# Input projection of a hybrid encoder kernel: from eight plain blocks to seven block products per set, with the steps between them reordered

## What is computed

```python
h = (_rmsnorm(x, g_mix) * (1.0 + scale1) + shift1).astype(dt)
proj = jnp.einsum('bsd,de->bse', h, w_in)
q, k, v, g_sw, p, gate_a, gate_b = jnp.split(proj, IN_SPLITS, axis=-1)
...
ret = ((ret - mu) * lax.rsqrt(var + EPS)).reshape(b, s, RET_V) * ret_gn_gain
branch_a = jax.nn.silu(g_sw) * ret
...
merged = jax.nn.sigmoid(gate_a) * branch_a + jax.nn.sigmoid(gate_b) * branch_b
mix_out = jnp.einsum('bsd,de->bse', merged.astype(dt), w_out)
x = x + gate1 * mix_out
...
up = _dwconv_centred(jnp.einsum('bsd,df->bsf', h2, w_up), conv_w, conv_b)
act, lin = jnp.split(up, 2, axis=-1)
return x + gate2 * jnp.einsum('bsf,fd->bsd', jax.nn.gelu(act) * lin, w_down)
```

## Time and profile before

| | us |
|---|---|
| median of 3 runs | 2647.01 (2646.71 to 2648.02) |
| span of the profiled execution | 2646.8 |
| TensorE busy in it | 2594.0 (98%) |
| DVE, ACT, POOL busy | 1659.9 (63%), 988.5 (37%), 1258.2 (48%) |
| the eight head pairs (all of `mix`) | 27.0 to 608.4 and 1337.8 to 1904.3 |

### The profile page before, as it was taken

One profiled execution on the slowest core, in us unless ns is written; L12 is line 12 of the kernel. 1 busy time (PEld: TensorE's weight loads), 2 busy tenths in 40 slices (PEclk: granted clock), 3 DMA queues, 4 the chain that ended last, 5 costly groups with the idle time before them and its releaser, 6 DMA issues.

```text
span 2646.8 us, 32184 instructions
## 1 busy us (share of the span) xinstructions
PE 2594.0 (98%) x12084; PEld 2131.5 (81%) x12084; DVE 1659.9 (63%) x2179; ACT 988.5 (37%) x1431; POOL 1258.2 (48%) x844
## 2 busy tenths in 40 slices
PE   7999989999999999999999999999999999999998
PEld 4888878888778888878878888888887888888886
DVE  3768686867786666665848273645768655555434
ACT  5211111114555454555621111111246545455443
POOL 1222333216377777655642122122453877775645
PEclk9999999999999999999999999999999999999998
DMA  7223153435134544497631212131251333325764
GB/s 297 91 88 125 48 197 112 150 112 154 58 128 147 167 168 158 157 337 238 184 122 49 70 33 85 33 92 43 81 147 32 104 120 104 103 93 180 213 193 146
DMA packets 300090, 341.01 MB, mean 129 GB/s; under 512 B 16288, under 2 KB 189728, under 8 KB 299936
## 3 DMA queue, kind: packets, MB, share of 16 engines
q1 hardware_dynamic: 297056, 328.46, 38.2%
q10 hardware_dynamic: 2880, 10.49, 1.0%
HBM read 263.39 MB, written 75.50 MB: 128 GB/s over the span
## 4 chain that ended last, share of the span: by engine, by line
PE 87%; DVE 5%; ACT 2%; DMA 2%; issue 2%; POOL 1%; SPq 1%; POOLq 0%; DVEq 0%; ACTq 0%
PE ps L921 26%; PE ps L890 23%; PE ps L1082 14%; PE ps L1247 11%; PE ps L977 5%; PE ps L1014 1%; PE ps L1275 1%; PE ps L1300 1%; PE ps L1299 1%; PE ps L1125 1%; PE ps L1312 1%; POOL y_sq L1823 1%; PE ps L1286 1%; DVE sq L2050 0%; ACT h_full L1492 0%
## 5 line engine op out<-in xcount | busy, mean ns | idle before, releaser
L1848 POOL TENSOR_TENSOR f_w<-f_ring,f_w 128x512 fp32r<-128x512 f32 x434 | 595.7, 1379 | 398.8 <-ACT f_w L1450 393.7
L921 PE MATMUL ps<-hc_hi,f_w 128*128 128x512 f32 x2240 | 690.5, 389 | 3.5 <-ACT u_act L1526 2.8
L1804 POOL TENSOR_TENSOR w_split<-w_raw,w_split 128x1024 fp32r<-128x1024 f32 x88 | 224.0, 2549 | 666.3 <-ACT w_split L1371 666.3
L890 PE MATMUL ps<-h_hi,w_split 128*128 128x512 f32 x1792 | 497.0, 394 | 6.9 <-ACT v_sb L1637 6.9
L921 PEld LDWEIGHTS ps<-hc_hi,f_w 128*128 128x128 f32 x2240 | 420.1, 188 | 92.7 <-ACT u_act L1526 3.7
L921 PE MATMUL ps<-hc_lo,f_w 128*128 128x512 f32 x1120 | 435.7, 389 | 0.0
L1082 PE MATMUL ps<-act_ring,f_w 128*128 128x512 f32 x1848 | 421.5, 390 | 3.6 <-DVE act_ring L2164 1.9
L1082 PEld LDWEIGHTS ps<-act_ring,f_w 128*128 128x128 f32 x1848 | 346.6, 188 | 77.5 <-issue 4.2
L890 PEld LDWEIGHTS ps<-h_hi,w_split 128*128 128x128 f32 x1792 | 334.2, 188 | 79.0 <-ACT v_sb L1637 7.5
L1450 ACT ACTIVATE f_w<-f_ring 128x512 fp32r<-128x512 f32 x434 | 269.9, 624 | 252.8 <-POOL f_ring L1858 109.7
L1247 PE MATMUL ps<-w_split,h_hi 128*128 128x512 f32 x1024 | 322.7, 396 | 5.5 <-DVE h_lo L2037 5.5
(11 more groups left out here) (210 smaller groups left out, 3296.7 us busy)
## 6 DMA issues: line engine op xcount, KB each, us to landing
f_ring<-in_w_up SPq DMA_DIRECT2D x160, 256.0 KB, 3.2
f_ring<-gated_out SPq DMA_DIRECT2D x154, 256.0 KB, 3.0
w_raw<-in_w_in SPq DMA_DIRECT2D x56, 512.0 KB, 3.9
gated_out<-gated_up SPq DMA_DIRECT2D x44, 512.0 KB, 4.1
f_ring<-down_sums SPq DMA_DIRECT2D x88, 256.0 KB, 3.0
gated_out<-t_gated SPq DMA_DIRECT2D x22, 768.0 KB, 6.0
f_ring<-in_w_down SPq DMA_DIRECT2D x66, 256.0 KB, 3.5
late_rows<-in_w_late SPq DMA_DIRECT2D x32, 512.0 KB, 5.6
```

Of the source, the lines that this page charges most:

```text
L890: ins = pe.matmul(ps[:, slot, b * HALF:(b + 1) * HALF], w[:, w_slot, col:col + P], a[:, k, b * HALF:(b + 1) * HALF], start=first and n == ...
L921: ins = pe.matmul(ps_row[:, half_of(bank)], a[:, cols], b, start=i in (0, 1, 3) and k == 0 and n == 0, stop=k == KQ - 1 and n == 2, skip_g ...
L1804: pool.tensor_tensor(w_lo[:, ws, :], w_raw[:, i % 2, :], w_hi[:, ws, :].bitcast(F32), ALU.subtract).then_inc(lo_done.sem, 1)
L1848: pool.tensor_tensor(piece_slot(q)[:, 1, :], piece_raw(q), piece_slot(q)[:, 0, :].bitcast(F32), ALU.subtract).then_inc(piece_lo.sem, 1)
```

## The change

The input projection is made in seven block products too, the order of everything in `mix` is rewritten around them, and weights and late rows are loaded otherwise.

1. *Gates.* GS, GA and GB become three *sets* (0: swish, 1: gate a, 2: gate b), each for both heads at once: the set's 256 output channels and the 1024 tokens are cut in 2x2 blocks, and seven products (`unit_product`, 12 matmuls of 512 columns each; (s, o) is product o of set s) take the place of 2 x 48 matmuls. Four products are copied out of PSUM by ACT (`copy_unit`: o = 0, 1, 2, 6; 512 columns), three are added on top by DVE (`unit_add(s, n)` after o = 3, 4, 5). The tanh is then taken from SBUF.
2. *q, k, v.* In pairs 1 to 3 of each sequence also in seven products (`qkv_products`, o = 0 to 6), 48 matmuls of 256 columns each; ACT copies four (`copy_qkv`), DVE adds three (`qkv_add`, 1024 columns). Rope then works on SBUF, in two halves (`rope_half`). In pair 0 q, k and v stay plain, and there the sums of blocks of h are made (`t_piece_low`, `t_piece_diff`, 2048 columns, DVE; `t_piece_high`, ACT).
3. *Order.* P comes right behind q, k, v; the turns of q and k behind P; the scores behind product (0, 0); the other small steps behind the products that the table `behind` names. DVE's and ACT's lists are rewritten in the same order.
4. *Weights.* 22 loads of 256 KB a pair through a ring of eight; 512-column pieces through five buffers; POOL also makes four sums of weight blocks per set. W_in comes with its columns permuted beforehand.
5. *Late rows.* Each sequence now sums its own 32 tiles, one instruction a tile, in its pairs 1 and 2, 16 tiles a pair, spread over six spots (`LATE_SPOTS`) of DVE's list; the ring has two buffers. Before, sequence 1 had none in its pairs.
6. *Around it.* x is loaded again ahead of `out` in both sequences, the first loads of `out` wait for the end of the last pair, and the block sums of w_out are made on POOL in pair 3 of sequence 0.

The core of the diff:

```diff
-LATE_RING = 4
-LATE_FROM = (0, 0, 10, 21, 32)
+LATE_RING = 2
+LATE_FROM = (0, 0, 16, 32, 32)
+LATE_SPOTS = (6, 3, 1, 2, 2, 2)
...
+            def late_load(seq, n):
                 if n >= LATE_RING:
-                    sp.wait_ge(late_sum, 2 * (n - LATE_RING) + 2)
+                    sp.wait_ge(late_sum, LATE_TILES * seq + n - LATE_RING + 1)
...
+                    for j in range(KC):
+                        mix_in(where, j)
...
+                    late = late_loads(late, 1)
+                    store_merged(("mix", seq, pr - 1))
+                    late = late_loads(late, LATE_SPOTS[0] - 1)
...
+                    for j in range(KC, KC + 4):
+                        mix_in(where, j)
...
+                    late = late_loads(late, sum(LATE_SPOTS[1:3]))
+                    for j in range(KC + 4, MIX_LOADS - 4):
+                        mix_in(where, j)
...
+            def qkv_products(where):
...
+                for o in range(PRODUCTS):
+                    i = ORDER_UP[o]
...
+                    elif o == 6:
+                        pe.wait_ge(*q_summed.at(where, 2))
+                    else:
+                        pe.wait_ge(*q_copied.at(where, {2: 1, 4: 3, 5: 2}[o]))
...
+                            rows, cols = slice(t * P, (t + 1) * P), slice(k2 * 2 * P, (k2 + 1) * 2 * P)
+                            k = 2 * kk + k2
+                            for n, (a, b) in enumerate(((high, w[0]), (high, w[1]), (low, w[0]))):
+                                ins = pe.matmul(ps[:, Q_SLOT[i], t * 2 * P:(t + 1) * 2 * P], a[:, k, rows], b[:, cols],
...
+            def pool_unit(where, between=None):
...
+                if pr:
+                    pe.wait_ge(*q_copied.at(where, 4))
...
+            def unit_product(where, s, o):
...
+                else:
+                    pe.wait_ge(*u_copied.at(where, 4 * s + {2: 1, 4: 3, 5: 2}[o]))
...
                     def branch_b(h):
                         slot = slot_of(where, f"BB{h}")
-                        if h == 0:
-                            pe.wait_ge(*cent_done.at(where, 1))
-                        else:
-                            pe.wait_ge(*sw_done.at(where, 2))
+                        pe.wait_ge(*ma_done.at(where, h + 1))
...
+                    if pr:
+                        qkv_products(where)
+                        pool_unit(where)
+                        turn_qk()
+                        behind = {(0, 2): (products, 0), (0, 4): (products, 1), (0, 6): (outputs, 0), (1, 3): (outputs, 1),
+                                  (1, 5): (turn_ret, 0), (2, 1): (branch_b, 0), (2, 3): (turn_ret, 1), (2, 4): (branch_b, 1)}
...
+            def copy_unit(where, s, o):
...
+                elif (s, o) == (2, 1):
+                    act.wait_ge(*ga_done.at(where, 2))
...
+                    def unit_add(s, n):
...
+                        dve.wait_ge(*used.at(where, set_piece(pr, s, 3 + n) + 1))
+                        dve.wait_ge(*u_copied.at(where, 4 * s + n + 1))
...
+                        late(0)
+                        qkv_add(0)
+                        rope_half(0)
+                        late(1)
+                        qkv_add(1)
+                        late(2)
+                        qkv_add(2)
+                        rope_half(1)
...
+                    unit_add(2, 0)
+                    normed(1)
+                    gate_a(1)
+                    unit_add(2, 1)
+                    branch_a(1)
+                    unit_add(2, 2)
```

1387 lines of the change are left out of this document (877 added, 510 removed), and 3 rows, old and new, of the table STEPS.

## The result

The changed kernel takes 2780.35 us (median of 4 runs, 2776.4 to 2783.07), the kernel before 2646.86 in the same comparison: a ratio of 1.050, 95% interval 1.0487 to 1.0516. It is slower by 133.5 us. The prediction had the sign, at 2670.0, but its range ended at 2705.

What follows compares the result with a forecast made beforehand. The prediction took TensorE, busy for 2594.0 of 2646.8 us, as the bound. 2646.8 less 93.7 us saved plus 116.9 us of new waits and lower clock gave 2670.0 us, with a range of 2605 to 2705.

Steps and rivals of the forecast that it cites:

- A: Pool unit waits for the copy of the last q, k, v product: 1.15 us in six pairs, 6.9 us.
- D: BB1 behind product (2, 4) waits for branch_a of head 1: 2.1 us in six pairs, 12.6 us.
- F: Start of out: its first loads and x wait for the end of the last pair, 4.5 us twice, 9 us.
- C: End of the gates: DVE's norm and gate_a of head 1 delay ACT's copies; 5.2 us in eight pairs, 41.6 us.
- B: Outputs of head 1 behind (1, 3) wait for the decayed q: 0.8 us late in six pairs, 4.8 us.
- E: Late rows in pairs 1 and 2 delay the second add of q, k, v: 6.5 us in four pairs, 26 us.
- G: Block sums of w_out on POOL in pair 3 of sequence 0 delay weight pieces: 3 us.
- H: Pair 0: block sums of h on DVE lie between rope and turns, 4.5 us twice, 9 us.
- lower clock: Lower clock after the late-row pause: 1 us a pair in four pairs, 4 us.
- Rival 4: Half clock again and again: 20 pauses of 5 us or more add 2 us each, 40 us, 2710; chance 0.13.
- Rival 1: Waits overlap and late rows keep up, with landings near 3.2 us: costs of 74 us, 2627; chance 0.28.
- Rivals 2, 3 and 5: Nothing waits, 2553 to 2575, chance 0.05; 256-column matmuls at 0.112 us, 2654, 0.13; at 0.188 us, 2807, 0.03.

Runs made afterwards that it cites:

- e11_pool_twice: The kernel before, with each of the 88 low parts of w_in computed twice on POOL: 2698.3 us, ratio 1.020.
- e5_pair0: The changed kernel with rope's first products and the copy of v ahead of the first block-sum piece of h in pair 0: 2780.9 us, ratio 1.051.
- e1_late_out: The changed kernel without the 64 late tiles in its pairs, their loads and the waits for them: 2713.9 us, ratio 1.025.
- e12_best: The changed kernel with end-of-pair adds moved, late tiles respread, head 1 outputs later, merged store first, pair 0, w_out and out-load orders changed: 2634.6 us, ratio 0.9952.
- e8_before_pause: The kernel before, with q, k, v of pairs 1 to 3 started only when DVE has merged head 1 of the pair ahead: 2679.3 us, ratio 1.013.

## Why the prediction was wrong, point by point

**Right.** The step of 256 columns, 0.120 us; with it, within some us, the saving of 84.5. Nearly all places of new waits. The wait of the pool unit (A: 6.8 us), BB1 (D: 11.8 for 12.6), the start of `out` (F: 11.9 for 9). The end of the gates (C) was a wait as described, but smaller: 16.2 for the turn of head 1 and 13.6 for the copy, 29.8 in place of 41.6. The norm took 1.61 us on average and not 2.29, which is 5.4 of the 11.8 (8 x 0.68); the rest isn't traced.

**Too small in the sum:**

| step of the sum | predicted | measured |
|---|---|---|
| B, outputs of head 1 | 4.8 | 14.7 |
| E, late rows, waits | 26 | 47.2 |
| G, pair 3 of sequence 0 | 3 | 5.8 |
| H, pair 0 | 9 | 29.4 |
| lower clock | 4 | 59.8 |
| other slow work | 0 | 8.4 |

These terms (A 6.8, B 14.7, C 29.8, D 11.8, E 47.2, F 11.9, G 5.8, H 29.4) are 157.4 us; the view's sum rose by 150.1, since before's own wait of 6.9 went and others moved a little.

1. *The clock.* This is the step that failed most: a term of 4 us measured 59.8. I took one us a pair in four pairs, from the one pause of the trace of before that was long. Rival 4 had the size, 40 us, and I gave it 0.13, against it above all that of before's pauses only the one of 6.9 us was followed by a low clock. That was a wrong reading. The earlier trace rows has one row of its view only and ends at 1340, and two short pauses of before do have one behind them, of 1.4 us at 1358.6 and of 1.2 at 696.4 (windows of work behind them; PEclk is the third figure from the end):

```profile
1361.50:1364.90 3.40, 3.40 (x10) 2.66 (x9) 2.51 (x4) 0.00 (x0) 0.86 (x1) 0.50 0.10 38
699.30:702.70 3.40, 3.40 (x10) 2.63 (x9) 2.65 (x6) 2.92 (x5) 0.33 (x1) 0.51 0.52 154
```

Others as short (1.7 at 52.3, 1.4 at 769.6) don't, so a short pause costs it sometimes. At the end of the changed kernel's pairs, with two or three pauses near each other, it comes every time: 5.5 to 8.8 us of work at 0.50, eight times of eight. The range should have held this price for every place that I had myself listed as a pause.
2. *E*, 47.2 for 26. The ring of two did what I had said, but DVE came to it late, at 17.7, 15.2, 17.6 and 15.2 us after the start of the four pairs and not at 11.2. That is 5.2 on average, and the wait was 5.3 longer than I took. I had priced the tables of the pair (the operations on 16 to 128 columns) at their lengths in before's quick pairs: 2.2 us there, 6.2 to 6.4 here. The merged sums took about as long as before in two of the four pairs and 2.1 us more in the other two. The row to look at was the spread of one group's durations, and pair 2 of sequence 0, where before itself starts at 17.0. That POOL's work beside them is the reason is argued from e11_pool_twice and that pair, not shown in the changed kernel.
3. *H.* In pair 0 I priced the extra operations by a guess of what remained uncovered (4.5 us a pair; it was 14.7, for the pool unit, the turns, KV0 and a product of set 1). Rows of before gave 59 us free on DVE, but after its share before the turns is full. e5_pair0 shows it: moving one step moved the wait.
4. *B.* The states and the swish of head 1 stand ahead of the decayed q; I had it 0.8 late where it was 2.6 or 2.7 in five of the six pairs. The decayed q itself was quicker than my price (1348 ns for 1738). Two late tiles stand ahead of it in the pairs that have them; without them, in e1_late_out, the six waits are 9.9 us and not 14.7. Where the rest comes from stays open, since the walk on record gives no terms.

The prediction's mechanism for the waits, places in DVE's queue rather than its load, was right; its price for the clock was not, and by that and by E and H the time left the range.

Rival 1 (late rows keep up, 2627) was wrong for this kernel. That e12_best, with other orders, comes near its number at 2634.6 doesn't confirm it: that run still has 94.1 us of waits. Rivals 2, 3 and 5 fall with the pair lengths and the step of 0.120.

What stays open: why some short pauses are followed by half clock and others aren't; whether the 8.4 us are restarts after a wait; and which POOL operation slows which DVE operation.

## What to carry to other kernels

A TensorE that is 98% busy hides nothing: price a change that trades matmuls for work on other engines by the pauses that it makes, each at its length and with the half clock that followed here, 1.7 to 3.0 us lost behind one of 4 us and 2.7 to 4.4 around three of 2 us, and not by the load of the other engines. When two or three steps that TensorE needs stand in one engine's queue among steps that it doesn't need, put those first; moving two adds in DVE's list was worth 56 us here, the same late tiles in other spots of the queue 38 more. And follow the DMA queue: a store behind a load that waits for a sum held up rope for 7.7 us, although all its data were ready.

## What the runs showed of the hardware

- Six pauses of 4 us in solid work on TensorE were each followed by 3.4 to 5.9 us of work at 0.50 of the clock (e8_before_pause), pauses of 10.5 to 12.8 us by 3.6 to 6.0 (changed kernel). So the longer pause didn't cost more clock behind it: 1.7 to 3.0 us lost for the one, 1.8 to 3.0 for the other. Three pauses of 2 us close together cost 2.7 to 4.4. In the kernel before, two single pauses of 1.2 and 1.4 us were followed by 3.4 us at half clock, and others of 1.4 and 1.7 weren't.
- A 256-column fp32r matmul with its own load of a stationary block goes every 0.120 us, a 512-column one every 0.227: the short form costs 6% more per column.
- With more work for POOL alone (e11_pool_twice) DVE operations on SBUF took longer, 950 to 2356 ns for a merged sum, but not all of them (norm 2294 and 2235). Two operations on 128 columns took 0.48 us in the kernel before in one pair, 2.50 in another beside a busy POOL, and 2.56 in the changed kernel. Those with a PSUM input kept their time: 1217 and 1218 ns for 1024 columns of L2471, 687 and 688 for the 512-column adds.
